# A hybrid decoder layer on one core: alternating two phases' groups, moving the samples' value loads and score transposes, and writing out the matmul engine's loops

## The chip, the cores and the metric

One Trainium2 chip; the program uses one of its cores. The metric is the device time of one execution in microseconds, as the median of several. The engines go by these names: PE is the matmul engine (TensorE; PEld is its weight load), DVE is VectorE, ACT is ScalarE, POOL is GpSimd, SP is the engine that only issues DMAs here.

## What is computed

One step of a decoder layer for 256 prompt tokens and 8 sample tokens that share all weights, T = 264 token columns in all:

```python
h = rmsnorm(x, norm_mix)
parts = jnp.split(h @ w_in, IN_SPLITS, axis=-1)     # u, b_gate, c_gate, q/k/v x 3, gate_a, gate_b
branch_a = (b_gate * causal_dwconv(c_gate * u)) @ w_conv_out
att = attend(qs, ks, vs)                            # samples: over 8 sequences' cached keys and values
branch_b = att.reshape(n, t, ATT_W) @ w_attn_out
x = x + (jax.nn.sigmoid(gate_a) * branch_a + jax.nn.sigmoid(gate_b) * branch_b) @ w_out
h = rmsnorm(x, norm_ffn)
up, gate = jnp.split(h @ w_ffn_in, 2, axis=-1)
x = x + (jax.nn.silu(causal_dwconv(gate) + ffn_conv_b) * up) @ w_ffn_down
```

D_MODEL is 2048, D_CONV 1024, ATT_W 512, D_FF 5632, everything in float32. The new keys, values and convolution states are outputs too.

## The kernel before

**Tiling.** All weights stream once through a ring. The unit is a *chunk*: 256 rows by 512 columns of a weight matrix, 512 KB, in a ring of RING = 4 slots. SP loads it into `raw` (`load`, L292). ACT rounds it to `w_hi` (`hi`, L351, the instruction is on L355), DVE makes the rest `w_lo = raw - w_hi` (`lo`, L550, instruction on L553), and PE multiplies it (`chunk`, L907): for each of four column tiles and two row halves three matmuls of 264 columns (L917 to L919), 24 in a chunk. `his` and `los` run AHEAD = 3 chunks in front of PE. `hi` waits for the landed chunk and for a free slot (`slots_free`, one up for each chunk that PE has finished), `lo` for `hi_ready`, PE for `lo_ready`, and SP's load of chunk s for the split of chunk s - 4.

**Groups.** A *group* is the chunks that make 512 output columns, so four tiles of the accumulator `acc`: eight chunks where the input has 2048 rows (N_MODEL), four for the convolution's output (N_CONV), two for the attention's output (N_ATT). PE can begin a group's tile m only when DVE (or ACT) has taken tile m of the group before (`psum_free`). `take_tiles` (L560) takes tile 0, splits one more chunk, and then takes tiles 1 to 3. The table PHASES (L61) fixes the order of the phases; each engine's program follows it by hand.

**Around the change**, in order of time:

- `ucb`, 48 chunks, written out on all engines; prompt attention is spread between them.
- `gate_a`, four groups in a loop of each engine. In each, DVE also does the samples' scores for two of the eight sequences (L743 to L751): two products and two sums of 1.2 us each over cached keys `k_a`, `k_b` and queries `q_a`, `q_b`. POOL loads them (`load_keys`, L1174, eight DMAs) once the scores of the group before are done, and right behind them the values of the same two sequences (`load_values`, L1185, four DMAs), L1200 to L1203. Behind each group ACT does the sigmoid.
- PE turns the scores (L1041, L1042) as soon as they are complete, before the first group of `conv_out`. DVE and ACT make the softmax of them (L754 to L761, L469).
- `conv_out`, four groups; before the last one PE turns the probabilities back (L1048).
- The samples' attention output: 64 small matmuls with each of `v_a`, `v_b` (L1057).
- `gate_b`, four groups; then `attn_out`, four groups of two chunks. For each of these DVE takes four tiles times `gate_b` into `tf` (L803) and adds `gate_a` (L807), ACT rounds it to `t_hi` (L487), POOL subtracts to `t_lo` (L1211).
- `w_out`, which reads `t_hi` and `t_lo`; then the FFN in two halves (`ffn_a`, `down_a`, `ffn_b`, `down_b`).

On PE all phases but `ucb`, the first third of `qkv` and `attn_out` are in loops (`fetched_loop`, L281): the body stands once in the code and the engine branches back.

Of the kernel before, what the change touches and what calls it, by code (L numbers as in the profile page):

```python
# [26 lines left out]
ALU = mybir.AluOpType  # L27
# [4 lines left out]
D_MODEL = 2048  # L32
# [29 lines left out]
          ("gate_b", 4, N_MODEL), ("attn_out", 4, N_ATT), ("w_out", 4, N_MODEL),  # L62
# [8 lines left out]
CHUNKS = _c  # L71

# [27 lines left out]
def trunk_program(nc, x_fm, w_in, w_conv_out, w_attn_out, w_out, w_ffn_in, w_ffn_down, params, rope_tab,  # L100
                  masks, ident_in, st_mix_in, st_ffn_in, caches, q_new, kv_new,
                  y_out, p_kv, s_kv, conv_state_out, ffn_state_out):
    with ExitStack() as ctx:
# [185 lines left out]
        def _(sp):  # L289
# [34 lines left out]
            with sp.Fori(0, 4) as i:  # L324
                group(w_in, N_MODEL, GW * i + (gate_col + D_MODEL), 2 * i + QUAD0["gate_b"])
            with sp.Fori(0, 2) as i:
                group(w_attn_out, N_ATT, 2 * GW * i, i + QUAD0["attn_out"])
                group(w_attn_out, N_ATT, 2 * GW * i + GW, i + QUAD0["attn_out"], s0=N_ATT)
# [21 lines left out]
        def _(act):  # L350
# [121 lines left out]
            with fetched_loop(mybir.EngineType.Activation, 0, 3) as i:  # L472
                his(i + QUAD0["conv_out"], 0, N_CONV)
# [6 lines left out]
            his(3 + QUAD0["conv_out"], 0, N_CONV)  # L480
            with fetched_loop(mybir.EngineType.Activation, 0, 3) as i:
                gate("gate_b", i, gate_b, gate_b_ready)
            gate("gate_b", 3, gate_b, gate_b_ready, early=1)
# [5 lines left out]
            for j in range(4):  # L489
                if j:  # L490
                    his(QUAD0["attn_out"], N_ATT * j, N_ATT * j + 1)
                    mix_hi(j - 1)
                his(QUAD0["attn_out"], N_ATT * j + 1, N_ATT * (j + 1))
# [55 lines left out]
        def _(dve):  # L549
# [203 lines left out]

            dve.wait_ge(sturned, 2)  # L754
# [7 lines left out]
            with fetched_loop(mybir.EngineType.DVE, 0, 4) as i:  # L762
                los(i + QUAD0["conv_out"], 0, N_CONV - 1)
                dve.wait_ge(gate_a_ready, 4)

                def take_a(m):
                    wait_tile(dve, i + GROUP0["conv_out"], i + QUAD0["conv_out"], N_CONV, m)
                    dve.tensor_tensor(tiles(gate_a, 4 * i + m), acc[:, m:m + 1, 0:T], tiles(gate_a, 4 * i + m),
                                      ALU.mult).then_inc(psum_free, 1)

                take_tiles(take_a, i + QUAD0["conv_out"], N_CONV - 1)
            los(QUAD0["gate_b"], 0, 7)
# [18 lines left out]
            los(2 * 3 + QUAD0["gate_b"], 4, N_MODEL - 1)  # L791
            take_gate("gate_b", 3, gate_b)
            for j in range(4):
                los(QUAD0["attn_out"], N_ATT * j, N_ATT * (j + 1) - 1)
                g = GROUP0["attn_out"] + j
                if j == 0:
                    dve.wait_ge(gate_b_ready, 4)
                if j >= 2:
                    dve.wait_ge(t_ready, j - 1)

                def take_mixed(m):
                    wait_tile(dve, g, QUAD0["attn_out"], N_ATT * (j + 1), m)
                    dve.tensor_tensor(tf[:, j % 2, m, :], acc[:, m, 0:T], gate_b[:, 4 * j + m, :], ALU.mult).then_inc(psum_free, 1)  # L803
# [505 lines left out]
```

## Time and profile before

| | |
|---|---|
| median of 3 runs | 1541.17 us (1539.62 to 1542.80) |
| profiled execution | 1545.92 us, its span 1544.1 us |
| PE busy | 98% |
| DVE, ACT, POOL busy | 58%, 45%, 5% |
| moved by DMA | 307.78 MB, 199 GB/s |
| 512 KB weight load of w_in, issue to landing | 4.1 us (median) |

The span is from the first instruction to the last; the time holds 1.8 us around it. A *busy* PE is one with a matmul in its pipeline; successive matmuls overlap. The *waits* view says for each engine what it stood idle for, and who released it; "issue" means that the profile shows nothing that it waited for. Line numbers are those of the kernel; where a helper records every operation, many phases share one line and are told apart by the tiles' names and by time. The *timeline* lists instructions in order of time, with the idle time before each in brackets. The *windows* view gives the busy time of each engine in a stretch, PE's granted clock (1.00 is 2.4 GHz, 0.50 is 1.2 GHz) and the busy share of the 16 DMA engines.

### The profile page before, as it was taken

What the parts mean: (1) busy time and instruction counts of PE and PEld (TensorE: products, weight loads), DVE (VectorE), ACT (ScalarE), POOL (GpSimd) and SP (SyncE); (2) the same over time, 40 slices, a digit from 0 to 9 for tenths busy, and PEclk for the clock granted to TensorE, in tenths of its full rate; (3) what the DMA queues carried; (4) which work ended last, traced back from release to release, by engine and by line L of the source; (5) the groups of instructions that cost most, each with busy time, mean ns of one, the idle gap of its engine ahead of it and who ended that gap; (6) DMA issues with size and microseconds to landing.
All of it is one profiled execution on the core that took longest, in us unless ns stands there. A gap on an engine that the chain in (4) does not pass through costs nothing.

```text
span 1544.1 us, 32221 instructions
## 1 busy us (share of the span) xinstructions
PE 1514.0 (98%) x12450; PEld 1508.2 (98%) x12450; DVE 893.1 (58%) x1056; ACT 693.0 (45%) x761; POOL 76.3 (5%) x144
## 2 busy tenths in 40 slices
PE   8999999999989999999999999999999999999997
PEld 8999999999988999999999999999999999999996
DVE  8646555756656544675665565663444656556554
ACT  7444444434444344444454444443333444444452
POOL 2000001001230000110000000000000000000000
PEclk9999999999999999999999999999999999999999
DMA  8867576556887665545577776775556565566552
GB/s 278 276 182 247 179 224 189 153 161 198 253 243 207 200 197 170 167 153 200 181 243 250 232 225 219 251 237 169 182 179 179 175 188 180 173 183 195 181 178 97
DMA packets 145108, 307.78 MB, mean 199 GB/s; under 512 B 10112, under 2 KB 10240, under 8 KB 144528
## 3 DMA queue, kind: packets, MB, share of 16 engines
q1 hardware_dynamic: 139120, 268.73, 56.6%
q0 software_dynamic: 5920, 38.12, 7.6%
q8 instruction: 47, 0.77, 0.2%
q14 instruction: 21, 0.17, 0.0%
HBM read 301.39 MB, written 26.38 MB: 212 GB/s over the span
## 4 chain that ended last, share of the span: by engine, by line
PE 95%; DVE 2%; DMA 1%; issue 1%; ACT 1%; SPq 0%; DVEq 0%; ACTq 0%
PE acc L917 31%; PE acc L918 31%; PE acc L919 31%; DMA raw<-w_in 1%; DVE w_lo L553 1%; PE side L1010 1%; PE side L989 1%; ACT w_hi L355 0%; DVE yg L894 0%; PE side L1001 0%; PE side L1057 0%; DVE gate_a L730 0%; DVE tf L803 0%; PE side L976 0%; DVE tf L807 0%
## 5 line engine op out<-in xcount | busy, mean ns | idle before, releaser
L553 DVE TENSOR_TENSOR w_lo<-raw,w_hi 128x1024 fp32r<-128x1024 f32 x503 | 616.8, 1235 | 535.2 <-ACT w_hi L355 532.8
L355 ACT ACTIVATE w_hi<-raw 128x1024 fp32r<-128x1024 f32 x503 | 529.5, 1058 | 728.9 <-PE acc L919 664.2
L917 PE MATMUL acc<-h_hi,w_hi 128*128 128x264 f32 x2872 | 823.6, 287 | 5.9 <-DVE gate_a L730 3.8
L918 PE MATMUL acc<-h_lo,w_hi 128*128 128x264 f32 x2872 | 818.2, 285 | 2.1 <-issue 2.1
L919 PE MATMUL acc<-h_hi,w_lo 128*128 128x264 f32 x2872 | 817.7, 285 | 0.0
L917 PEld LDWEIGHTS acc<-h_hi,w_hi 128*128 128x128 f32 x2872 | 541.3, 188 | 8.2 <-DVE gate_a L730 4.8
L918 PEld LDWEIGHTS acc<-h_lo,w_hi 128*128 128x128 f32 x2872 | 541.4, 189 | 2.4 <-issue 2.3
L919 PEld LDWEIGHTS acc<-h_hi,w_lo 128*128 128x128 f32 x2872 | 541.5, 189 | 0.0
L917 PE MATMUL acc<-f_hi,w_hi 128*128 128x264 f32 x704 | 201.3, 286 | 3.5 <-issue 3.5
L918 PE MATMUL acc<-f_lo,w_hi 128*128 128x264 f32 x704 | 200.8, 285 | 0.0
L919 PE MATMUL acc<-f_hi,w_lo 128*128 128x264 f32 x704 | 200.7, 285 | 0.0
L917 PEld LDWEIGHTS acc<-f_hi,w_hi 128*128 128x128 f32 x704 | 133.0, 189 | 3.7 <-issue 3.7
L918 PEld LDWEIGHTS acc<-f_lo,w_hi 128*128 128x128 f32 x704 | 132.9, 189 | 0.0
L919 PEld LDWEIGHTS acc<-f_hi,w_lo 128*128 128x128 f32 x704 | 132.9, 189 | 0.0
L917 PE MATMUL acc<-t_hi,w_hi 128*128 128x264 f32 x256 | 73.0, 285 | 0.9 <-DVE tf L803 0.9
L918 PE MATMUL acc<-t_lo,w_hi 128*128 128x264 f32 x256 | 72.8, 284 | 0.0
L919 PE MATMUL acc<-t_hi,w_lo 128*128 128x264 f32 x256 | 72.8, 284 | 0.0
L917 PEld LDWEIGHTS acc<-t_hi,w_hi 128*128 128x128 f32 x256 | 48.1, 188 | 1.1 <-DVE tf L803 1.1
L919 PEld LDWEIGHTS acc<-t_hi,w_lo 128*128 128x128 f32 x256 | 48.1, 188 | 0.0
L918 PEld LDWEIGHTS acc<-t_lo,w_hi 128*128 128x128 f32 x256 | 48.1, 188 | 0.0
L918 PE MATMUL acc<-ab_lo,w_hi 128*128 128x264 f32 x128 | 37.0, 289 | 1.0 <-issue 1.0
L917 PE MATMUL acc<-ab_hi,w_hi 128*128 128x264 f32 x128 | 37.5, 293 | 0.5 <-DVE gate_a L730 0.4
(186 smaller groups left out, 841.1 us busy)
## 6 DMA issues: line engine op xcount, KB each, us to landing
raw<-w_in SPq DMA_DIRECT2D x183, 512.0 KB, 4.1
raw<-w_ffn_in SPq DMA_DIRECT2D x176, 512.0 KB, 4.2
raw<-w_ffn_down SPq DMA_DIRECT2D x88, 512.0 KB, 4.5
raw<-w_out SPq DMA_DIRECT2D x32, 512.0 KB, 4.6
s_kv<-cache POOLq DMA_DIRECT2D x16, 1020.0 KB, 8.8
raw<-w_conv_out SPq DMA_DIRECT2D x16, 512.0 KB, 4.7
raw<-w_attn_out SPq DMA_DIRECT2D x8, 512.0 KB, 3.8
s_kv<-cache POOLq DMA_DIRECT2D x8, 508.0 KB, 5.0
```

Of the source, the lines that this page charges most:

```text
L355: act.activation(w_hi[:, s % RING], raw[:, s % RING], ACT.Copy).then_inc(hi_ready, 1)
L553: dve.tensor_tensor(w_lo[:, s % RING], raw[:, s % RING], w_hi[:, s % RING].bitcast(F32), ALU.subtract).then_inc(lo_ready, 1)
L917: pe.matmul(out, w_hi[:, slot, k, cols], backwards(m_hi[:, kt + k, :]), start=first and k == 0, stop=False)
L918: pe.matmul(out, w_hi[:, slot, k, cols], backwards(m_lo[:, kt + k, :]), start=False, stop=False)
L919: mm = pe.matmul(out, w_lo[:, slot, k, cols], backwards(m_hi[:, kt + k, :]), start=False, stop=last and k == 1)
L989: mm = pe.matmul(side[:, SCORES + n * g:SCORES + n * (g + 1)], qkv[:, 12 * g + h, P * qt:P * (qt + 1)], qkv[:, 12 * g + 4 + h, 0:n], start ...
L1010: mm = pe.matmul(side[:, HEAD_OUT:HEAD_OUT + P], vtok[:, kb, (g * HEADS + h) * HEAD_DIM:(g * HEADS + h + 1) * HEAD_DIM], prob_t[:, P * b:P ...
```

## The change

PHASES gets one phase `mix` in place of `gate_b` and `attn_out`. Its eight groups run in the order of WOVEN: second gate 0 and 1, attention 0, gate 2, attention 1, gate 3, attention 2 and 3. SP, ACT, DVE and PE follow this order, written out. A sum is rounded (`mix_hi`) after three chunks' rounding of the next gate group.

In `conv_out`, PE turns the scores behind group 0 and the probabilities behind group 1 (before: ahead of group 0 and behind group 2). DVE does its softmax steps behind group 0, ACT its exponential after five chunks.

POOL loads in the first gate's phase only keys and queries, beside the values of batch 0; batch 1 of the values follows the last scores, batches 2 and 3 follow PE's end of convolution groups 0 and 1.

All loops of PE are written out. The number of matmuls, of bytes and of weight chunks is the same.

```diff
-          ("gate_b", 4, N_MODEL), ("attn_out", 4, N_ATT), ("w_out", 4, N_MODEL),
+          ("mix", 8, (N_MODEL + N_ATT) // 2), ("w_out", 4, N_MODEL),
...
+WOVEN = (("gate_b", 0), ("gate_b", 1), ("attn_out", 0), ("gate_b", 2), ("attn_out", 1), ("gate_b", 3),
+         ("attn_out", 2), ("attn_out", 3))
+MIX_AT = {}
+_c = 0
+for _n, (_name, _j) in enumerate(WOVEN):
+    MIX_AT[_name, _j] = (GROUP0["mix"] + _n, QUAD0["mix"] + _c // RING, _c % RING)
+    _c += N_MODEL if _name == "gate_b" else N_ATT
+assert QUAD0["mix"] + _c // RING == QUAD0["w_out"]
...
+            for name, j in WOVEN:
+                _, quad, s0 = MIX_AT[name, j]
+                if name == "gate_b":
+                    group(w_in, N_MODEL, GW * j + (gate_col + D_MODEL), quad, s0=s0)
+                else:
+                    group(w_attn_out, N_ATT, GW * j, quad, s0=s0)
...
+            his(QUAD0["conv_out"], 0, N_CONV + 1)
             act.wait_ge(smax_ready, 1)
...
+            his(QUAD0["conv_out"], N_CONV + 1, 2 * N_CONV)
             act.wait_ge(pt_zeroed, 2)
             act.wait_ge(spt_done, 2)
...
+            his(QUAD0["conv_out"], 2 * N_CONV, 4 * N_CONV)
...
+            def gate_b_group(j, begun, to_round=None):
+
+                g, quad, s0 = MIX_AT["gate_b", j]
+                if to_round is not None:
+                    his(quad, s0 + begun, s0 + 3)
+                    begun = 3
+                    mix_hi(to_round)
+                his(quad, s0 + begun, s0 + N_MODEL + 1)
+                wait_taken(act, g, TILES - 1)
+                act.activation(gate_b[:, 4 * j:4 * j + 4, :], gate_b[:, 4 * j:4 * j + 4, :], ACT.Sigmoid).then_inc(gate_b_ready, 1)
+
+            def attn_out_group(j, begun):
+                _, quad, s0 = MIX_AT["attn_out", j]
+                his(quad, s0 + begun, s0 + N_ATT)
+
+            gate_b_group(0, 0)
+            gate_b_group(1, 1)
+            attn_out_group(0, 1)
+            gate_b_group(2, 0, to_round=0)
+            attn_out_group(1, 1)
+            gate_b_group(3, 0, to_round=1)
+            attn_out_group(2, 1)
+            his(MIX_AT["attn_out", 3][1], MIX_AT["attn_out", 3][2], MIX_AT["attn_out", 3][2] + 1)
+            mix_hi(2)
+            attn_out_group(3, 1)
...
+            dve.wait_ge(gate_a_ready, 4)
+            conv_group(0)
             dve.wait_ge(sturned, 2)
             dve.tensor_scalar(sprob[:, :], side[0:BATCH * HEADS, 0:SAMPLE_KEYS], -SCALE, None, ALU.mult).then_inc(snegated, 1)
             dve.wait_ge(snegated, 1)
             dve.tensor_reduce(ssmall[:, 0:1], sprob[:, :], AX_X, ALU.min).then_inc(smax_ready, 1)
+            los(QUAD0["conv_out"], N_CONV, N_CONV + 1)
...
+            conv_group(1, begun=1)
+            conv_group(2)
+            conv_group(3)
...
+            def attn_out_group(j):
+                g, quad, s0 = MIX_AT["attn_out", j]
+                los(quad, s0, s0 + N_ATT - 1)
+                dve.wait_ge(gate_b_ready, j + 1)
+                if j >= 2:
+                    dve.wait_ge(t_ready, j - 1)
...
+            gate_b_los(0, 0, 4)
             dve.wait_ge(base_ready, 2)
             dve.wait_ge(shead_done, 1)
             dve.tensor_copy(srows[:, :], side[:, 1024:1024 + HEAD_DIM]).then_inc(srows_ready, 1)
-            take_gate("gate_b", 0, gate_b)
-            with fetched_loop(mybir.EngineType.DVE, 1, 3) as i:
-                los(2 * i + QUAD0["gate_b"], 0, N_MODEL - 1)
-                take_gate("gate_b", i, gate_b)
-            los(2 * 3 + QUAD0["gate_b"], 0, 4)
-
+            gate_b_los(0, 4, N_MODEL - 1)
+            take_gate_b(0)
+            gate_b_los(1, 0, 4)
             dve.wait_ge(sturned_back, 1)
...
-            los(2 * 3 + QUAD0["gate_b"], 4, N_MODEL - 1)
-            take_gate("gate_b", 3, gate_b)
...
+            gate_b_los(1, 4, N_MODEL - 1)
+            take_gate_b(1)
+            attn_out_group(0)
+            gate_b_los(2, 0, N_MODEL - 1)
+            take_gate_b(2)
+            attn_out_group(1)
+            gate_b_los(3, 0, N_MODEL - 1)
+            take_gate_b(3)
+            attn_out_group(2)
+            attn_out_group(3)
...
-            with fetched_loop(mybir.EngineType.PE, 1, NG) as g:
+            for g in range(1, NG):
...
-            with fetched_loop(mybir.EngineType.PE, 0, 4) as i:
+            for i in range(0, 4):
                 h_run(2 * i + QUAD0["gate_a"], i + GROUP0["gate_a"])
+            nbh = BATCH * HEADS
+
+            def conv_group(i):
+                run(i + QUAD0["conv_out"], i + GROUP0["conv_out"], N_CONV, ab_hi, ab_lo)
+
+            pe.wait_ge(ab_ready, 2)
+            conv_group(0)
             pe.wait_ge(scored, 8)
-            pe.transpose(side[0:BATCH * HEADS, 0:ROWS_A], sc_a[:, :], ident[0:ROWS_A, 0:ROWS_A]).then_inc(sturned, 1)
-            pe.transpose(side[0:BATCH * HEADS, ROWS_A:SAMPLE_KEYS], sc_b[:, :], ident[0:ROWS_B, 0:ROWS_B]).then_inc(sturned, 1)
-            pe.wait_ge(ab_ready, 2)
-            with fetched_loop(mybir.EngineType.PE, 0, 3) as i:
-                run(i + QUAD0["conv_out"], i + GROUP0["conv_out"], N_CONV, ab_hi, ab_lo)
+            pe.transpose(side[0:nbh, 0:ROWS_A], sc_a[:, :], ident[0:ROWS_A, 0:ROWS_A]).then_inc(sturned, 1)
+            pe.transpose(side[0:nbh, ROWS_A:SAMPLE_KEYS], sc_b[:, :], ident[0:ROWS_B, 0:ROWS_B]).then_inc(sturned, 1)
+            conv_group(1)
             pe.wait_ge(sprob_ready, 1)
-            nbh = BATCH * HEADS
             pe.transpose(side[0:ROWS_A, 512:512 + nbh], sprob[:, 0:ROWS_A], ident[0:nbh, 0:nbh]).then_inc(spt_done, 1)
             pe.transpose(side[0:ROWS_B, 544:544 + nbh], sprob[:, ROWS_A:SAMPLE_KEYS], ident[0:nbh, 0:nbh]).then_inc(spt_done, 1)
-            run(3 + QUAD0["conv_out"], 3 + GROUP0["conv_out"], N_CONV, ab_hi, ab_lo)
+            conv_group(2)
+            conv_group(3)
...
+            gate_b_group(0)
             pe.wait_ge(srows_ready, 1)
             pe.transpose(side[:, 0:P], srows[:, :], ident[:, :]).then_inc(sturned_back, 1)
-            h_run(2 * 3 + QUAD0["gate_b"], 3 + GROUP0["gate_b"])
+            gate_b_group(1)
             pe.wait_ge(att_ready, 2 * HEADS)
             pe.wait_ge(satt_ready, 1)
-            for j in range(4):
-                run(QUAD0["attn_out"], GROUP0["attn_out"] + j, N_ATT, att_hi, att_lo, s0=N_ATT * j)
-            with fetched_loop(mybir.EngineType.PE, 0, 4) as i:
+            attn_out_group(0)
+            gate_b_group(2)
+            attn_out_group(1)
+            gate_b_group(3)
+            attn_out_group(2)
+            attn_out_group(3)
+            for i in range(0, 4):
...
             ffn_pair("a", 0, stats=1)
-            with fetched_loop(mybir.EngineType.PE, 1, PAIRS_A) as i:
+            for i in range(1, PAIRS_A):
                 ffn_pair("a", i)
-            with fetched_loop(mybir.EngineType.PE, 0, 2) as i:
+            for i in range(0, 2):
                 down("a", i, N_DOWN_A, 0)
-            with fetched_loop(mybir.EngineType.PE, 0, PAIRS_B) as i:
+            for i in range(0, PAIRS_B):
                 ffn_pair("b", i)
-            with fetched_loop(mybir.EngineType.PE, 0, 2) as i:
+            for i in range(0, 2):
                 down("b", i, N_DOWN_B, PAIRS_A)
...
-            with pool.Fori(1, 4) as i:
+            for i in range(1, 4):
                 pool.wait_ge(scored, 2 * i)
                 load_keys(i)
+            pool.wait_ge(scored, 8)
+            load_values(1)
+            for i in range(2, 4):
+                pool.wait_ge(slots_free, RING + 4 * QUAD0["conv_out"] + N_CONV * (i - 1))
                 load_values(i)
 
 
-            pool.wait_ge(slots_free, RING + 4 * QUAD0["gate_b"])
+            pool.wait_ge(slots_free, RING + 4 * QUAD0["mix"])
```

## Rows read from the trace of the kernel before

**Rows 1.** Page, its span, and busy time by engine: share, instructions
```profile
span 1544.1 us, 32221 instructions
...
PE 1514.0 (98%) x12450; PEld 1508.2 (98%) x12450; DVE 893.1 (58%) x1056; ACT 693.0 (45%) x761; POOL 76.3 (5%) x144
```

**Rows 2.** Waits of PE: line <- releaser: us in total, times, longest
```profile
PE acc L917 <- DVE gate_a L730: 4.2, 4, 2.8
PE acc L917 <- issue: 4.0, 2, 3.5
PE acc L918 <- issue: 3.1, 2, 2.1
PE acc L917 <- DVE tf L803: 2.1, 3, 0.9
PE side L1041 <- DVE sc_b L749: 1.8, 1, 1.8
PE acc L917 <- DVE w_lo L553: 1.5, 2, 1.2
```

**Rows 3.** Timeline of PE: start, us, instruction [idle before it <- releaser]
```profile
453.82 0.28 PE L919 MATMUL acc<-h_hi,w_lo 128*128 128x264 f32 x1
...
456.93 0.39 PE L917 MATMUL acc<-h_hi,w_hi 128*128 128x264 f32 x1 [2.82 <-DVE gate_a L730]
...
484.59 0.28 PE L1041 MATMUL side<-ident,sc_a 128*32 128x128 f32 x1 [1.80 <-DVE sc_b L749]
...
612.37 0.49 PE L918 MATMUL acc<-h_lo,w_hi 128*128 128x264 f32 x1 [2.07 <-issue]
...
1043.12 0.59 PE L917 MATMUL acc<-f_hi,w_hi 128*128 128x264 f32 x1 [3.46 <-issue]
```

**Rows 4.** Windows: length, PE, PEld, DVE, ACT, POOL busy (x), PEclk, DMA share, GB/s
```profile
225.00:376.00 151.00, 151.00 (x1242) 150.38 (x1241) 91.86 (x139) 66.43 (x86) 12.71 (x25) 1.00 0.62 185
388.00:405.00 17.00, 17.00 (x142) 17.00 (x142) 12.78 (x12) 6.36 (x6) 2.67 (x6) 1.00 0.84 252
458.90:462.30 3.40, 3.40 (x18) 3.40 (x17) 0.13 (x1) 3.05 (x3) 3.05 (x7) 0.50 0.81 233
1047.00:1180.00 133.00, 133.00 (x1098) 133.00 (x1098) 60.12 (x59) 48.72 (x46) 0.00 (x0) 1.00 0.57 175
```

**Rows 5.** Timeline of POOL, loads of the third key and value batch
```profile
433.80 0.51 POOL L1183 DMA_DIRECT2D q_b<-q_new  x1
...
436.54 0.58 POOL L1190 DMA_DIRECT2D v_b<-kv_new  x1 [0.21 <-issue]
```

**Rows 6.** DMA issues, window 430 to 450: KB each, us to landing
```profile
raw<-w_in SPq DMA_DIRECT2D x5, 512.0 KB, 10.6
...
q_b<-q_new POOLq DMA_DIRECT2D x1, 12.0 KB, 10.3
...
v_b<-kv_new POOLq DMA_DIRECT2D x1, 12.0 KB, 11.7
```

**Rows 7.** Timeline of ACT, window 448 to 449
```profile
448.56 1.06 ACT L355 ACTIVATE w_hi<-raw 128x1024 fp32r<-128x1024 f32 x1 [7.54 <-DMA raw<-w_in]
```

**Rows 8.** Timeline of DVE, windows 456 to 457 and 486 to 492
```profile
456.46 0.42 DVE L730 TENSOR_TENSOR gate_a<-acc,r 128x264 f32 x1
...
491.51 0.15 DVE L759 RECIPROCAL ssmall<-ssmall 32x1 f32<-32x1 f32 x1 [3.81 <-ACT sprob L470]
```

**Rows 9.** Timeline of DVE and POOL, window 645 to 649
```profile
646.62 2.40 DVE L553 TENSOR_TENSOR w_lo<-raw,w_hi 128x1024 fp32r<-128x1024 f32 x1
...
645.49 2.44 POOL L1211 TENSOR_TENSOR t_lo<-tf,t_hi 128x1056 fp32r<-128x1056 f32 x1 [109.03 <-ACT t_hi L487]
```

**Rows 10.** Instruction queue: packets, MB, share; page, then 226:376 and 1038:1090
```profile
q8 instruction: 47, 0.77, 0.2%
...
q8 instruction: 9, 0.15, 0.4%
...
q8 instruction: 5, 0.08, 0.6%
```

More of the change, by code:

```diff
@@ L752, in _, with conv_group, take_a @@
                 take_gate("gate_a", i, gate_a)
+            def conv_group(i, begun=0):
+                quad = QUAD0["conv_out"]
+                los(quad, N_CONV * i + begun, N_CONV * (i + 1) - 1)
+                def take_a(m):
+                    wait_tile(dve, i + GROUP0["conv_out"], quad, N_CONV * (i + 1), m)
+                    dve.tensor_tensor(tiles(gate_a, 4 * i + m), acc[:, m:m + 1, 0:T], tiles(gate_a, 4 * i + m),
+                                      ALU.mult).then_inc(psum_free, 1)
+                take_tiles(take_a, quad, N_CONV * (i + 1) - 1)
+            dve.wait_ge(gate_a_ready, 4)
+            conv_group(0)
             dve.wait_ge(sturned, 2)
@@ L761, in _, with take_gate_b, take, gate_b_los @@
             dve.tensor_scalar(sprob[:, :], sprob[:, :], ssmall[:, 2:3], None, ALU.mult).then_inc(sprob_ready, 1)
[L762 to L772, printed above, removed]
+            conv_group(1, begun=1)
+            conv_group(2)
+            conv_group(3)
+            def take_gate_b(j):
+                g, quad, s0 = MIX_AT["gate_b", j]
+                def take(m):
+                    wait_tile(dve, g, quad, s0 + N_MODEL, m)
+                    dve.tensor_tensor(gate_b[:, 4 * j + m, :], acc[:, m, 0:T], r[:, :], ALU.mult).then_inc(psum_free, 1)
+                take_tiles(take, quad, s0 + N_MODEL - 1)
+            def gate_b_los(j, first, last):
+                _, quad, s0 = MIX_AT["gate_b", j]
+                los(quad, s0 + first, s0 + last)
+            def attn_out_group(j):
[4 more added lines that the diff above has]
+                    dve.wait_ge(t_ready, j - 1)
+                def take_mixed(m):
+                    wait_tile(dve, g, quad, s0 + N_ATT, m)
+                    dve.tensor_tensor(tf[:, j % 2, m, :], acc[:, m, 0:T], gate_b[:, 4 * j + m, :], ALU.mult).then_inc(psum_free, 1)
+                take_tiles(take_mixed, quad, s0 + N_ATT - 1)
+                wait_taken(dve, g, TILES - 1)
+                dve.tensor_tensor(tf[:, j % 2], tf[:, j % 2], gate_a[:, 4 * j:4 * j + 4, :], ALU.add).then_inc(mixed, 1)
+            gate_b_los(0, 0, 4)
             dve.wait_ge(base_ready, 2)
@@ L1060, in _, with gate_b_group, attn_out_group @@
             mm.then_inc(shead_done, 1)
[L1061 to L1062 removed]
+            def gate_b_group(j):
+                g, quad, s0 = MIX_AT["gate_b", j]
+                h_run(quad, g, s0=s0)
+            def attn_out_group(j):
+                g, quad, s0 = MIX_AT["attn_out", j]
+                run(quad, g, N_ATT, att_hi, att_lo, s0=s0)
+            gate_b_group(0)
             pe.wait_ge(srows_ready, 1)
             pe.transpose(side[:, 0:P], srows[:, :], ident[:, :]).then_inc(sturned_back, 1)
[L1065 removed]
+            gate_b_group(1)
             pe.wait_ge(att_ready, 2 * HEADS)
             pe.wait_ge(satt_ready, 1)
[L1068 to L1070 removed]
+            attn_out_group(0)
[5 more added lines that the diff above has]
+            for i in range(0, 4):
                 run(2 * i + QUAD0["w_out"], i + GROUP0["w_out"], N_MODEL, t_hi, t_lo,
```

31 lines of the change are left out of this document (removed).

## The prediction

> **What bounds the kernel now.** I read the page first. The matmul engine is busy for 98% of the span and no other engine for more than 58% [rows 1]; the chain that ended last is 95% matmuls. So only two things can shorten this kernel: fewer matmuls, or fewer pauses between them. The change leaves every matmul in place, so I counted the pauses. Second view: the waits of the matmul engine [rows 2]. They sum to 16.7 us in six lines, and the list is short enough to place each one in time with the engine's timeline [rows 3]. Two conversions are needed. A matmul is listed with 0.28 us but the next one starts 0.12 us after it, so a listed idle time is 0.16 us short of what is lost: 453.82 to 456.93 is 3.11 us, 2.99 more than the usual 0.12, and 2.82 are listed [rows 3]. And after the longer pauses the granted clock is at half: from 458.9 to 462.3 the window shows 0.50 (the 1.2 GHz level), with 18 matmuls, those at its edges counted, where full speed (1098 in 133 us, 0.121 us each) has 28 [rows 4]. Some 16 matmuls take 3.4 us instead of 1.9, so 1.5 us per such stretch. There are four: behind the pauses that end at 456.93 and 458.40, at 484.59 and 486.40, at 612.37, and at 1043.12. The six lines with their 14 pauses' 0.16 us each, and the four stretches, are 16.7 + 2.2 + 6.0 = 24.9 us: about that is what any reordering can win. 1.2 us of w_lo and 0.5 us of issue in them lie in the first 36 us, which the change doesn't touch.
>
> **The change part by part.**
>
> *Values' loads.* In each of the first gate's groups 1 to 3, GpSimd issues eight key and query loads and behind them four value loads, 844 KB; in group 2 the last of the first kind at 433.80, the last of the second at 436.54 [rows 5]. They sit in the same 16 DMA engines as the weights. In 430 to 450 us a 512 KB weight load takes 10.6 us to land; the last value load lands 11.7 us after its issue, at 448.2 [rows 5, 6]. ScalarE waits 7.54 us for that weight chunk and starts on it at 448.56 [rows 7]. VectorE then has three chunks to split and four key steps to do back to back, and comes to the gate's tiles only at 456.46 [rows 8]; the matmul engine has nowhere to write from 454 on. Without the values, what landed with and after the keys comes earlier by the values' own transfer. Bounds: 844 KB at the 252 GB/s that 388 to 405 carried is 3.3 us [rows 4]; the last value at 448.2 against the last query piece at 433.80 + 10.3 = 444.1 is 4.1 us [rows 5, 6]. I take 4.1, as it is measured between two landings. VectorE is then at the gate's first tile at 452.4, a tile that the matmul engine needs at 453.9, so the 2.99 us go, and with them the smaller pauses around it. Listed idle of this stage: three of the four "gate_a" waits (4.2 less the 0.42 of 486.40) and 0.27 of w_lo, 4.1 us; plus 4 x 0.16 and 0.3 us of a pause too short to be listed: 5.0 us. Plus one half-clock stretch: 6.5 us. With 3.3 instead of 4.1 us some 0.8 us stays. Where the loads go: batch 1 now starts at the end of the key steps, batches 2 and 3 one and two groups into the convolution's output. There the price is bounded by the one place where a value batch runs without keys today: at 387 us; the matmul engine had no idle time in 388 to 405 [rows 4]. I take nothing, and the same 3 to 5 us as above as the other end. The last batch is issued two groups (23 us) ahead of its use and took at most 11.7 us to land, so the wait for the values stays empty. GpSimd's next job, the load of x, waits for the same point as before.
>
> *Score transposes later.* Today the matmul engine waits for the last score sum, starts the transposes at 484.59 after 1.80 us of listed idle, 1.97 lost, and then pauses twice more, for 0.85 us in all, for a tile that VectorE frees late [rows 2, 3]. With a group of the convolution (11.7 us) put in front, the score sums are long done: 1.97 + 0.85 + a half-clock stretch of 1.4 = 4.2 us. The two transposes still run. In the new order VectorE's softmax steps come after group 0: ScalarE's exponential holds VectorE for 3.81 us today [rows 8], but behind that wait is queued only the split of the chunk that group 2 starts with, some 11 us before it is needed; the probabilities are needed one group later too. Cost nothing; if that cover were missing, 3.8 us.
>
> *The matmul engine's loops written out.* Three pauses have no releaser ("issue"): 1.0 us in the convolution's loop, 2.07 us right after the second gate's loop is left (it ends at 612.37), 3.46 us right after the first FFN loop is left (it ends at 1043.12) [rows 2, 3]. The DMA queue of the instruction blocks (16 KB each) has 47 packets over the span: five of them in 1038 to 1090, just behind the first FFN loop [rows 10]. Straight code is in the trace too: the 48 chunks from 225 to 376 us take nine blocks in 151 us, which would be 91 over 1531 us, and the engine is busy for all of it [rows 4, 10]. So a loop that repeats fetches next to nothing, and the code behind it is fetched only when the loop is left, and whether that stalls depends on how much of it is already there. Written out, every block is fetched ahead like those: 1.0 + 2.07 + 3.46 + 3 x 0.16 = 7.0 us, and two half-clock stretches, 3.0: 10.0 us. The Trainium skill ("Runtime: NRT & Kernel Launch", section "Instruction fetch mechanics") has the same rule: the matmul engine's buffer is refilled in 16 KiB blocks ahead of use, purely in sequence, and a taken branch to a block that isn't there forces a fetch before execution goes on. The rows of the two loop exits agree. The 1.0 us inside the convolution's loop might by the rows alone be another's, and the sum 1.2 us less; by the rule it is a late block too.
>
> *Alternating groups.* An attention group has only two chunks, 5.8 us of matmuls. Four in a row leave VectorE no room: two splits, four tiles and a sum are 5.2 us when undisturbed, and a split beside GpSimd's subtraction (645.49 to 647.93) took 2.40 us instead of 1.23 [rows 9]. Three pauses follow, 2.1 us listed, 2.6 us in truth [rows 2]. Between groups of the second gate (eight chunks, 23.3 us, in which VectorE has eight splits of 1.23 us and four tiles) the rounding and GpSimd's subtraction fall where there is slack. The last two attention groups still stand together, with GpSimd's subtraction beside the second, so one pause of 0.5 us remains, now ahead of the output projection: 2.1 us gained. New waits: the first attention group needs the samples' attention after gate group 1 instead of 3; its steps are queued behind the fifth chunk of that group, some 9 us ahead. VectorE waits for each sigmoid by group, and each is at least one group old, but for the last, which has the third attention group as cover (5.8 us for about 3). Cost nothing.
>
> **Sum.** 6.5 + 4.2 + 10.0 + 2.1 = 22.8 us. Profiled execution 1545.92 us (span 1544.1 and 1.8 around it): 1523.1 us. The median of the runs shown is 4.75 us below the profiled one. Either recording costs that much outside the pauses, then it stays, 1518.4; or the unrecorded runs have less of the pauses, then part of the gain isn't there, 1523.1. I take the middle: 1520.5 us; its own range is 1516 to 1526.
>
> **The rivals.**
> 1. *The values disturb the convolution's output.* By the Trainium skill ("DMA: Bandwidth & Descriptors", section "Issuing engines are not separate DMA queues") loads of all issuers interleave on the same 16 engines, so moving one only moves the crowd. In this kernel: batch 1 is issued right behind the last keys' backlog, and the convolution's weights need 180 GB/s (512 KB in 2.9 us) with 72 GB/s more from the values (844 KB in 11.7 us). For it: the second gate-a group shows that a burst can cost 5 us. Against it: 252 GB/s was carried in 388 to 405 without a pause [rows 4]. Price: one pause of 3 us and a half-clock stretch, 4.5: 1525.
> 2. *The "issue" pauses are not the loops'*, or come back elsewhere. For it: nine loops are left, and only three pauses show. Price: the 10.0 us stay: 1530.5.
> 3. *Slower: straight code whose blocks come late.* Written out, the engine needs a block every 17 us all along, some 91 instead of 47, also under GpSimd's key loads with the DMA engines 0.8 busy and more; the straight code of 225 to 376 had them at 0.62 [rows 4]. A late block costs what the three did, 2 to 3.5 us and 1.5 for the clock, 4.2 on average. The rest of the change saves 12.8, so from 4 late blocks on the kernel is slower than before: with seven, 1541.2 - 12.8 + 29.4 = 1557.8. Against it: nine blocks without a wait, and each transfer took about 1 us.
> 4. *The woven groups pause*: a wait in front of or behind each lone attention group, the price of the largest pause there today, 1.1 us, four times: 2.1 gained become 2.3 lost: 1525.
>
> **How the numbers follow.** Forecast 0.70, rival 1 0.09, rival 2 0.10, rival 3 0.04, rival 4 0.04, other 0.03. The range goes from 1515.5 (all pauses gone and 3 us more beside the part that recording explains) to 1529 (rivals 1 and 4 in; rival 2 mostly out). A measurement of this kernel can tell about 0.2%, 3.1 us, from no change. Faster by more: all but rival 3 and part of "other", 0.93; within 0.03; slower 0.04.
>
> **What would show it.** In the changed kernel's profile: no "issue" waits of the matmul engine beyond the 0.5 us near 32 us, and 90 to 100 packets in the queue of the instruction blocks; no wait for gate_a tiles from the first gate on, ScalarE's waits for weights there down from 7.5 to about 3.5 us; the score transposes with no wait ahead; at most one wait for tf; and PEclk at 1.00 from 5 us to the end but for stretches that a pause explains. The prediction is wrong if the count of instruction blocks rises and "issue" waits rise with it, if weight loads in the convolution's output take over 9 us to land, or if the pauses vanish but the median falls by less than 15 us, which would mean that they belonged to the recording.

## The result, and the profile after

The changed kernel takes 1522.96 us (median of 4, 1521.77 to 1525.36) against 1541.99 us (4 runs, 1539.62 to 1544.24): 19.0 us less, ratio 0.9879, 95% interval 0.9859 to 0.9899. Profiled execution against profiled execution it is 1521.96 against 1545.92 us, 24.0 less. The prediction was 1520.5 us and, for the profiled one, 1523.1. One of all the runs below, of the changed kernel with its loops put back, took 2102.28 us at a mean granted clock of 0.65 against 1529 to 1532 us of its others, and is left out.

The page of the changed kernel, its span, engines, granted clock (tenths, 40 slices) and the queue of the matmul engine's instruction blocks:

```profile
span 1520.4 us, 31542 instructions
...
PE 1505.6 (99%) x12450; PEld 1502.7 (99%) x12450; DVE 891.6 (59%) x1056; ACT 686.7 (45%) x756; POOL 77.4 (5%) x144
...
PEclk9999999999999999999999999999999999999998
...
q8 instruction: 99, 1.62, 0.4%
```

The waits of PE in it (us in total, times, longest), complete. They answer to [rows 2], where six lines had 14 waits, the sc_b one among them (two more of the view, 1.3 and 0.9 us, lie in its first 12 us):

```profile
PE acc L971 <- DVE w_lo L581: 2.0, 1, 2.0
PE side L1014 <- POOL ones L1175: 1.3, 1, 1.3
PE acc L971 <- DVE tf L831: 0.4, 1, 0.4
```

The first two are the start, before 12 us. Between 36 us and the end one wait of 0.4 us is left, the one ahead of the output projection. The gate_a, sc_b and issue lines are gone, and with them all four half-clock stretches. The blocks fetched went from 47 to 99.

Where the time came from is seen in the first gate. ScalarE's wait for weights there, and VectorE's arrival at the tiles of groups 2 and 3 of the gate (timelines of ACT and DVE):

```profile
442.33 1.06 ACT L366 ACTIVATE w_hi<-raw 128x1024 fp32r<-128x1024 f32 x1 [2.57 <-DMA raw<-w_in]
...
449.10 1.21 DVE L777 TENSOR_REDUCE sc_b<-k_b 83x1024 f32 x1
450.51 0.43 DVE L758 TENSOR_TENSOR gate_a<-acc,r 128x264 f32 x1 [0.21 <-PE acc L973]
...
472.31 1.21 DVE L777 TENSOR_REDUCE sc_b<-k_b 83x1024 f32 x1
473.82 0.43 DVE L758 TENSOR_TENSOR gate_a<-acc,r 128x264 f32 x1 [0.30 <-PE acc L973]
```

Before, ScalarE waited 7.54 us [rows 7] and VectorE took the tile at 456.46 without having waited for it [rows 8]. Now it is VectorE that waits for the matmul engine, at 450.51 and at 473.82. The last score sum starts at 472.31 instead of 483.3, and the window shows no idle time at all in a stretch that still moves 252 GB/s (length, busy PE, PEld, DVE, ACT, POOL, granted clock, DMA share, GB/s):

```profile
425.00:490.00 65.00, 65.00 (x538) 64.97 (x538) 43.84 (x50) 33.65 (x32) 13.81 (x24) 1.00 0.86 252
```

The value batches now land under the convolution's output. In 487 to 512 us its weight loads take 6.3 us to land (median of six), more than the 4.7 of the kernel before (median of all sixteen), and the matmul engine has no wait there:

```profile
raw<-w_conv_out SPq DMA_DIRECT2D x6, 512.0 KB, 6.3
...
v_a<-cache POOLq DMA_DIRECT2D x2, 512.0 KB, 5.9
```

### The profile page after: what moved, and what is told of

Same layout as the page of the kernel before. It is cut to its first block, busy times and chain, and to the rows that moved or that the text cites. A ratio compares the mean times of both kernels' runs of the same rounds, so it can differ in the third digit from the quotient of the medians.

```text
span 1520.4 us, 31542 instructions
## 1 busy us (share of the span) xinstructions
PE 1505.6 (99%) x12450; PEld 1502.7 (99%) x12450; DVE 891.6 (59%) x1056; ACT 686.7 (45%) x756; POOL 77.4 (5%) x144
## 4 chain that ended last, share of the span: by engine, by line
PE 98%; DVE 1%; DMA 0%; SPq 0%; ACT 0%; issue 0%; DVEq 0%
PE acc L971 32%; PE acc L972 32%; PE acc L973 32%; PE side L1064 1%; PE side L1043 1%; DMA raw<-w_in 0%; DVE yg L948 0%; PE side L1055 0%; PE side L1116 0%; DVE w_lo L581 0%; PE side L1030 0%; DVE r L623 0%; PE side L1169 0%; ACT w_hi L366 0%; PE side L1002 0%; SPq L316 0%
```

## The experiments

The first two, the fourth and the fifth do one part of the change alone on the kernel before, the third does two parts together; then come two runs that move nothing but the place of the code, and parts undone. Each time is given beside runs of the kernel before on the same chip. These had medians of 1542.09, 1546.35 and 1545.12 us in the three series of these runs, so differences from different series can be off by some microseconds; the profiled executions all stand against the one of the kernel before, 1545.92.

### The loops written out, alone

```diff
-            with fetched_loop(mybir.EngineType.PE, 1, NG) as g:
+            for g in range(1, NG):
...
```

and likewise all others of PE.

> The kernel before with only the matmul engine's loops written out. Theory (the code behind a loop is fetched late): the three issue pauses of 1.0, 2.07 and 3.46 us and two half-clock stretches go, 8.5 to 10 us less than before in the profiled execution, some 99 instruction blocks instead of 47; the gate_a, sc_b and tf waits stay as they are. Rival (the pauses are not the loops'): they stay or move, and the time is within 2 us of before. Rival (straight code is fetched late where the DMA engines are full, 400 to 480 us, since keys and values are still loaded together here): new issue pauses of 2 to 3.5 us there.

Measured: 1535.71 us against 1542.09, ratio 0.9955 (0.9938 to 0.9973): 6.4 us less; profiled 1532.88, which is 13.0 below the 1545.92 of before. Its waits of PE:

```profile
PE acc L917 <- DVE gate_a L730: 4.3, 4, 2.9
PE acc L917 <- DVE tf L803: 2.1, 3, 0.9
PE acc L917 <- DVE w_lo L553: 1.9, 2, 1.5
PE side L960 <- POOL ones L1104: 1.3, 1, 1.3
PE acc L933 <- DVE w_lo L604: 0.3, 1, 0.3
PE acc L917 <- issue: 0.2, 1, 0.2
```

All three issue pauses behind loops are gone, none is new in 400 to 480 us, and the gate_a and tf lines are nearly those of [rows 2]. The sc_b wait is gone as well, though this edit doesn't touch it: the last sum began at 482.00 us instead of 483.33, and the matmul engine came some 0.7 us later, since its half-clock stretch in the gate was twice as long here (456.4 to 463.1 us, with 27 matmuls). That is 2 of the 3 us by which the profiled execution gained more than the 8.5 to 10 expected. So the pauses were the loops', and straight code isn't late even with keys and values on the DMA engines. The median moved less than the profiled execution did; that is taken up below.

### The values moved, alone

```diff
-            with pool.Fori(1, 4) as i:
+            for i in range(1, 4):
                 pool.wait_ge(scored, 2 * i)
                 load_keys(i)
+            pool.wait_ge(scored, 8)
+            load_values(1)
+            for i in range(2, 4):
+                pool.wait_ge(slots_free, RING + 4 * QUAD0["conv_out"] + N_CONV * (i - 1))
                 load_values(i)
```

> The kernel before with only the value batches 1 to 3 moved behind the scores and into the convolution's output. Theory (values hold up the weights): ScalarE's longest wait for weights in the first gate falls from 7.5 to about 3.5 us, the gate_a pauses (5.0 us) and the half-clock stretch behind them go, and part of the wait for the last score sum, since that comes 4 us earlier too: 6.5 to 10 us less. The issue pauses stay. Rival (the keys alone are enough to hold up the weights): the 2.82 us pause stays at over 1.5 us, under 4 us are gained. Rival (the values now disturb the convolution's output): a pause and half-clock stretch there, 4.5 us back.

Measured: 1538.43 us against 1542.09, ratio 0.9964 (0.9947 to 0.9981): 3.7 us less, and the profiled execution, 1543.33, only 2.6. Its waits of PE, and the instruction behind the longest:

```profile
PE acc L918 <- issue: 8.1, 2, 6.3
PE acc L917 <- issue: 3.6, 2, 3.2
PE acc L917 <- DVE w_lo L553: 2.6, 2, 1.4
PE acc L917 <- DVE tf L803: 2.2, 3, 0.9
PE side L960 <- POOL ones L1104: 1.3, 1, 1.3
```
```profile
486.43 0.38 PE L918 MATMUL acc<-ab_lo,w_hi 128*128 128x264 f32 x1 [6.34 <-issue]
```

No gate_a and no sc_b line: this part alone removes all of what I had booked under the values and under the score transposes. But the pause in the convolution's loop, 1.0 us before, is now 6.34 us, and a half-clock stretch of 6.8 us begins towards its end; so most of the gain is lost again. The trace has the instruction queue's packet, one of 16 KB. In the kernel before it goes from 488.59 to 489.47 us and the matmul engine goes on at 491.06. Here the last matmul starts at 479.81, the packet goes from 483.89 to 484.91, and the next matmul starts at 486.43. Value batch 1 was issued from 475 us on, and the packet starts just when the DMA engines have become empty (length, busy PE, PEld, DVE, ACT, POOL, granted clock, DMA share, GB/s):

```profile
480.00:483.80 3.80, 0.09 (x1) 0.00 (x0) 1.03 (x3) 3.17 (x5) 0.00 (x0) 1.00 0.88 189
483.80:486.00 2.20, 0.00 (x0) 0.00 (x0) 0.66 (x1) 0.00 (x0) 0.00 (x0) 0.74 0.18 40
```

That speaks for the block having stood in line behind the values; when it was asked for isn't in the trace. The convolution's output is disturbed then, as the first rival said, but by way of the code, not of the weights.

### Loops written out and values moved

> The kernel before with two parts together: the matmul engine's loops written out and the value batches moved. Apart they gave 6.4 us and 3.7 us. Theory (with loops, the value batch that now runs under the convolution's loop holds up that loop's late code block, 6.3 us; written out, the block is fetched ahead): no issue pause over 0.5 us, no gate_a pause, together 14 to 17 us less than before, more than the sum of 10.1. Rival (the parts just add up): 10 us. Rival (the values also delay blocks of straight code): issue pauses of over 1 us between 475 and 510 us.

Measured: 1524.62 us against 1546.35, ratio 0.9860 (0.9845 to 0.9875): 21.7 us less, twice the 10.1 of the two apart. Waits of PE, complete:

```profile
PE acc L917 <- DVE tf L803: 2.2, 3, 0.9
PE acc L917 <- DVE w_lo L553: 1.6, 1, 1.6
PE side L960 <- POOL ones L1104: 1.3, 1, 1.3
PE acc L933 <- DVE w_lo L604: 0.3, 1, 0.3
PE acc L917 <- issue: 0.3, 1, 0.3
```

More than I had expected, 14 to 17. Each part takes away what spoils the other: in the written-out code no block is late, so the values can't hold one up. The size of that surplus is less sure. The same kernel, run once more on the chip of the single parts, was 19.5 us below the kernel before. In the profiled executions the parts give 13.0 + 2.6 = 15.6 us apart and 21.6 together, and the 6.0 between them is near what the traces list: a code pause longer by 5.3 us and half-clock stretches worth 3.0 us that the single parts kept and the two together don't have, less the 2.0 us of the sc_b wait, which both single parts lost. What the medians show beyond that isn't explained.

### The scores' transposes moved, alone

On PE (the convolution's first group in front; the probabilities stay behind group 2), with VectorE's and ScalarE's order as in the change:

```diff
+            run(QUAD0["conv_out"], GROUP0["conv_out"], N_CONV, ab_hi, ab_lo)
             pe.wait_ge(scored, 8)
             pe.transpose(side[0:BATCH * HEADS, 0:ROWS_A], sc_a[:, :], ident[0:ROWS_A, 0:ROWS_A]).then_inc(sturned, 1)
...
-            with fetched_loop(mybir.EngineType.PE, 0, 3) as i:
+            with fetched_loop(mybir.EngineType.PE, 1, 3) as i:
```

> The kernel before with only the score transposes and the softmax steps put behind the convolution's group 0 (probabilities still turned behind group 2). Theory of the sum: the wait of 1.80 us for the last score sum goes, the pause for a gate_a tile at the first convolution group stays or grows, since VectorE is as late as before (its last score sum ends at 484.5 and the tiles of the gate come after it): 1 to 2 us gained, not 4.2. If the 4.2 us are this part's own: 3.5 us or more gained. Rival (VectorE's softmax steps in front of the next splits become late): a w_lo wait in the convolution's output, slower by 1 to 3 us.

Measured: 1534.89 us against 1542.09, ratio 0.9946 (0.9930 to 0.9962), 7.2 us less. By the time alone the second case, the part being worth 4.2 us of its own, would seem right. The waits of PE tell otherwise:

```profile
PE acc L926 <- DVE gate_a L730: 6.2, 5, 2.8
PE acc L926 <- DVE w_lo L553: 2.3, 2, 2.1
PE acc L926 <- DVE tf L812: 2.2, 3, 0.9
PE side L969 <- POOL ones L1114: 1.3, 1, 1.3
PE acc L942 <- DVE w_lo L604: 0.7, 1, 0.7
PE acc L926 <- issue: 0.3, 1, 0.3
```

The sc_b wait of 1.8 us has become a gate_a wait of about the same length (4.2 in [rows 2], 6.2 here). So the transposes' place took no pause away; at most the half-clock stretch goes to its credit that stood behind the sc_b wait (486.3 to 489.6 us) and isn't there in this run (granted clock 1.00 in 484 to 496 us). What fell is the 6.5 us of issue pauses, of which 0.3 is left. They stood behind the first gate's, the second gate's and the first FFN loop, which this edit doesn't touch. It takes one pass out of the convolution's loop and so puts 96 matmuls and their weight loads more into the code.

### The groups alternating, alone

The change's mix phase with everything else of the kernel before, PE's other loops included.

> The kernel before with only the second gate's and the attention output's groups alternating; their code is written out on all engines, all other loops of the matmul engine stay. Theory: of three tf pauses of 2.1 us listed one of about 0.4 stays, 2.1 us gained; and as the second gate's loop is gone, the issue pause of 2.07 us and its half-clock stretch go too, 3.8 us: about 6 us less than before. Rival (lone attention groups pause): tf or gate_b waits at each of them, only the 3.8 us gained or less.

Measured: 1538.48 us against 1542.09, ratio 0.9975 (0.9958 to 0.9992): 3.6 us less, where about 6 had been expected; the profiled execution is 7.6 us below. The tf line is down to one wait, as predicted, and with the second gate's loop its pause has gone. The pause behind the first FFN loop is still there, and that in the convolution's loop is 1.8 us instead of 1.0 (L963). The gate stage has its gate_a waits; the sc_b wait isn't there, as in the run with the loops, though neither touches what it waits for:

```profile
PE acc L962 <- DVE w_lo L581: 4.9, 2, 3.0
PE acc L962 <- DVE gate_a L758: 4.0, 3, 1.9
PE acc L963 <- issue: 1.8, 1, 1.8
...
PE acc L962 <- DVE tf L822: 0.4, 1, 0.4
```

The w_lo line hides the pause behind the first FFN loop, 3.46 us in the kernel before: at 1035.11 us the matmul engine had been idle for 3.01 us, and the view names a split that ended at 1034.65. But that one belongs to the chunk three further on; the one that the engine went on with was split before 1028.7.
### Nothing moved but the place of the code

The run with the scores alone made it a question why loops pause at all, so here nothing of the work is changed. 128, in another run 64 instructions that only count up an unused semaphore stand in front of PE's code:

```diff
             pe.sem_inc(psum_free, TILES)
+            for _ in range(128):
+                held(pe)
```

> The kernel before with 128 instructions that do nothing (an unused semaphore counted up) put in front of the matmul engine's code, half an instruction block. Theory (whether leaving a loop stalls depends on where its end lies in the blocks): the three issue pauses (1.0 us at 490, 2.07 at 612, 3.46 at 1043) change in size, or vanish, or come behind other loops; everything else stays, apart from a start that is later by the time of the 128. Rival (they belong to a place in the work, a semaphore or a DMA): the same three pauses within 0.5 us each at the same places.

> The kernel before with 64 instructions that do nothing in front of the matmul engine's code (half of the run with 128, where the start came 17.6 us later and, of the pauses at 490, 612 and 1043, none was left and one of 1.1 us stood 22 us into the third FFN phase's surroundings, at 1189). Theory (place of the code in the blocks): again another set of issue pauses, start some 9 us later. Rival (the late start, not the place of the code, took the pauses away): no set of its own, the same as with 128.

Each was run once: 1557.62 us with 128 (the kernel before: 1546.35 on that chip) and 1554.98 with 64 (1545.12). With 128 the start comes late (20.9 us of issue before the first matmul), and between 640 us and the end the waits of PE are

```profile
PE acc L919 <- DVE tf L803: 2.2, 3, 0.9
PE acc L920 <- issue: 1.1, 1, 1.1
```

The pauses of 1.0, 2.07 and 3.46 us are gone; one of 1.1 us stands at 1190.52, behind the first down projection's loop, which had none. With 64 there are three long ones, at the ends of the qkv loop and of the first FFN loop, and 3 us into the code behind the second FFN loop:

```profile
228.90 0.39 PE L919 MATMUL acc<-h_hi,w_hi 128*128 128x264 f32 x1 [2.38 <-issue]
...
1046.05 0.58 PE L919 MATMUL acc<-f_hi,w_hi 128*128 128x264 f32 x1 [4.08 <-DVE f_lo L865]
...
1426.33 0.29 PE L921 MATMUL acc<-f_hi,w_lo 128*128 128x264 f32 x1 [2.48 <-issue]
```

The 4.08 us are named after VectorE's `f_lo`, but the first chunk of the down projection needs only the first pair's, which was done 230 us earlier.

That another set of pauses isn't just another execution is seen from the runs whose matmul engine has the same code up to the pause: the kernel before, the run with the values alone and the one with the groups alone all pause at the same matmul of the convolution's first pass (for 1.0, 6.3 and 1.8 us), and the first two also at the same ones behind the second gate's and the first FFN loop (2.1 and 1.8, 3.5 and 3.2 us). So the place goes with the code, the length varies.

And what the engine lacks is in the traces. Fifteen pauses of 0.7 us and more stand behind loops in the traces of the kernel before, of the values alone, of the groups alone, of both padded kernels and of the loops put back. In each, one 16 KB packet of the instruction queue ended 1.3 to 1.9 us before the matmul that ended the pause.

So the pauses belong neither to a semaphore nor to a stage of the work, nor to a late start: they go with how the code lies in its blocks. That explains the issue pauses that came and went in the single parts. An edit that adds or removes instructions ahead of a loop can draw the pauses behind all later loops anew. The Trainium skill ("Runtime: NRT & Kernel Launch", section "Instruction fetch mechanics") says that a taken branch whose target isn't in the current window forces a fetch before execution can continue. The traces agree that a fetch is waited for; the fifteen pauses all came within 30 matmuls behind a loop's last pass, and none at a branch back. With 0, 64 and 128 instructions in front their sum is 6.5, 8.9 and 1.1 us with the same work.

### The loops put back into the changed kernel

> The changed kernel with the matmul engine's loops put back where the order of groups still allows them (first third aside: qkv, first gate, output projection, FFN and down projections). Theory: one or more issue pauses of 1 to 6 us, at the convolution behind the first gate's loop (the value batch lands there) and behind an FFN loop, each over 2 us with a half-clock stretch of 1.5 us: 4 to 10 us slower than the changed kernel, but in the traces with loops pauses come and go with the place of the code, so it can also hit none, then 0 to 1 us. Rival (loops cost nothing, other parts made the gain): within 1.5 us of the changed kernel and no issue pause.

Measured: 1529.21 to 1532.49 us against 1546.35, ratio 0.9896 (0.9880 to 0.9912) to the kernel before. The changed kernel stands at 0.9879 in one series and 0.9861 in another, so the loops cost 2.6 to 5.4 us here, at the lower end of the 4 to 10 expected; the interval still overlaps that of 0.9879. Two of their waits of PE, and the longest in its place, the end of the second FFN loop:

```profile
PE acc L971 <- issue: 4.1, 3, 3.0
...
PE acc L973 <- issue: 1.0, 1, 1.0
```
```profile
1395.76 0.39 PE L971 MATMUL acc<-f_hi,w_hi 128*128 128x264 f32 x1 [3.03 <-issue]
```

### The values put back into the changed kernel

> The changed kernel with the value batches back beside the keys in the first gate. Theory: gate_a or w_lo pauses of 4 to 5 us in all and a half-clock stretch between 425 and 485 us, 5 to 8 us slower than the changed kernel, and no issue pause, since straight code is fetched ahead even there. Rival (straight code is late where the DMA engines are full): issue pauses of over 1 us between 400 and 480. Rival (the late score sum was what mattered): under 3 us slower.

Measured: 1533.56 us against 1546.35, ratio 0.9920 (0.9907 to 0.9934), which is 6.3 us more than by the changed kernel's 0.9879 and 9 more than by its 0.9861; expected were 5 to 8. The waits of PE and the longest wait of ScalarE for weights:

```profile
PE acc L971 <- DVE gate_a L758: 6.4, 4, 2.8
...
PE acc L971 <- issue: 0.4, 1, 0.4
```
```profile
ACT w_hi L366 <- DMA raw<-w_in: 30.3, 17, 6.9
```

All the pauses of the gate stage return with the values, also the one ahead of the convolution's output, now named gate_a instead of sc_b, and two half-clock stretches with them. The 0.4 us of issue is the one near 32 us, as before the change: straight code, keys and values together, and no late block.

### The transposes put back; and the changed kernel beside it

> The changed kernel once more, on the chip of the next three, as their measure. All four parts. Expected 21 to 24 us below before on this chip, no issue pause over 0.5 us and one tf pause of 0.4 us.

> The changed kernel with the score transposes and the softmax steps back in their old places, the loops written out all the same. Theory formed from the run with loops and values alone, which had no wait for the last score sum: with the values out of the way that sum is done some 9 us before the transposes, so this part is worth nothing of its own; within 1 us of the changed kernel, no sc_b wait. Rival (the prediction's sum, in which the part has 4.2 us of its own): a pause of 1 to 2 us at the start of the convolution's output, and 3 us or more slower.

> The kernel before with loops written out and values moved, once more beside the changed kernel, so that what the other two parts add is measured on one chip. Theory: the two tf pauses of 0.9 us each and the small one moved elsewhere, 2.1 us; scores nothing: 1.5 to 2.5 us slower than the changed kernel. Rival (lone attention groups cost what they save): within 0.7 us.

Measured on one chip, where the kernel before takes 1545.12 us:

| kernel | us | ratio (95%) |
|---|---|---|
| the changed kernel | 1522.32 | 0.9861 (0.9843 to 0.9879) |
| with the transposes in their old place | 1523.35 | 0.9865 (0.9844 to 0.9886) |
| loops and values only | 1525.64 | 0.9884 (0.9865 to 0.9903) |

The second has no sc_b wait and no pause in the convolution's output; profiled it takes 1523.44 against the changed kernel's 1523.79. The transposes' place is worth nothing once the values are moved, or less than these runs can tell. The third is 2.3 us behind the second (1.1 in the profiled executions), about the size of the two tf waits and their 0.16 us each, though the intervals overlap, so the times alone don't show it. Its traces name those waits:

```profile
PE acc L917 <- DVE tf L803: 2.1, 3, 0.9
```

## Why the prediction was right, and where it wasn't

**What bounds the kernel, and the count of pauses.** Right. The matmul engine is still the bound, 24.9 us were counted as what reordering can win, and 23.7 us of span went.

**Values' loads, 6.5 us.** Right in mechanism, too small in size. ScalarE's wait fell from 7.54 to 2.57 us (2.63 at the longest in any group of the gate), VectorE came to the tile with time to spare, and the lower bound's left-over of 0.8 us didn't show. What was mis-sized is what hangs on it: the sc_b wait and the pauses behind it, listed under the next part, are gone with the values alone. With the loops written out the values are worth 8.6 us in the profiled executions (1532.88 to 1524.29), and put back they cost 10.7 there (1532.64 against 1521.96) and 6.3 to 9 by the ratios.

**Score transposes, 4.2 us.** The step that failed. The pauses at the start of the convolution's output came from the same cause as those of the gate: the last score sum was late because the weights were. With the values moved and the transposes in their old place, that sum starts at 473.80 us, takes 1.2, and the transposes run at 477.17 without a wait: 2 us to spare (the 9 us in that run's expectation were wrong). Alone, the transposes' move only turned the 1.8 us wait into a gate_a wait; undone, it changed nothing beyond 1 us. The sum stayed right because 6.5 + 4.2 = 10.7 us is about what the values gave, 8.6 to 10.7 profiled. That is luck: I had priced the second stage's pauses as if the first hadn't been mended, and gave them to a part that earns nothing. The sc_b wait isn't even steady: it was 1.8 us in the kernel before, 2.5 in both padded kernels and absent in the runs with the loops or the groups alone.

**Loops written out, 10.0 us.** Right for this profiled execution: all three pauses went, alone and in the whole, and 99 blocks were fetched, where 90 to 100 had been foretold. The 1.0 us in the convolution's loop, which the prediction left open by its rows, is a late block too: its packet ended 1.6 us before the matmul at 491.06. But the pauses are not a constant of the kernel before. Of the loops' part alone, 13.0 us show in the profiled execution and 6.4 us in the median. And I missed how this part and the values depend on each other: apart 6.4 and 3.7 us, together 21.7 and, on the other chip, 19.5.

**Alternating groups, 2.1 us.** Right by the traces: 2.1 us listed became 0.4, in the place and of the size foretold, and no wait stands at the lone attention groups. The 2.3 us between the two kernels that differ in it have the right size, but lie within the noise.

**Profiled execution and median.** The 4.75 us between them in the kernel before were split in the middle between "recording costs it" and "the pauses vary". What the runs show speaks for the second: in the runs before, times spread over 1536.8 to 1549.6 us, while the changed kernel's lie in 1521.8 to 1525.4, and its recorded runs are 1.0 us below and 1.5 above their medians. The mean granted clock of the 38 runs before in the three series goes with their times: the 16 at 0.992 and 0.993 took 1545.4 us on average, the two at 0.997 took 1537.0. So the number of half-clock stretches, and of pauses in front of them, differs from one execution to the next; with the pauses gone the spread is gone. Which pauses vary was seen in no second trace of the same kernel. An unrecorded run had less of them to lose: hence 19.0 us less in the median against 24.0 profiled, and 1523 instead of 1520.5.

**The rivals.** The first (values disturb the convolution's output) happens, but only with loops left in, and through a code block instead of weights: 6.34 us at its worst. The second (the issue pauses aren't the loops') falls with the loops' own run and the padded ones. The third (straight code late) falls: no issue wait over 0.5 us in 1500 us of straight code, even with the values back in the gate. The fourth is refuted by the tf line.

**Open.** Why a given place of a loop in the blocks pauses for 1.0, 2.07 or 3.46 us, and another doesn't, wasn't worked out; the three placements show only that it does, and each padded kernel has only one trace. Nor was the alternation tried with the transposes moved but the values not.

## What to carry to other kernels

Before adding up the pauses of a bound engine, ask of each which earlier one made it: two of mine had one cause, and the sum was right only since both went. A loop on the engine that sets the time can stall at its end by some microseconds, at a place that any edit to the code ahead of it moves, and longer when a burst of other DMA stands in front of the missing block; where the program isn't too long, write that engine's loops out before measuring anything else, or each measurement carries that draw. And put bulk loads into a stage where the ring of weights has no other bulk load beside it, rather than right behind the keys that the same stage waits for.

## What the runs showed of the hardware

- Behind a loop's end the matmul engine paused for 0.7 to 4.1 us until an instruction block was there, and for 6.3 us with 844 KB of value loads in the DMA engines. The block's packet took 0.9 to 1.1 us, and the next matmul started 1.3 to 1.9 us after it. In straight code, with 99 such 16 KB blocks, there was no such pause.
- 128 semaphore increments in front of the matmul engine's code delayed its first matmul until 20.9 us after its start, 64 until 11.1 us: by the difference 0.15 us each.
- VectorE's split next to GpSimd's subtraction takes 2.40 us instead of 1.23 in the changed kernel too. By the alternation two of GpSimd's four subtractions (at 587.57 and 616.72 us) run beside groups of the gate, where nobody waits. This split is the one beside the last attention group, and the one wait left, 0.4 us at 644.76, comes behind it:

```profile
641.97 2.40 DVE L581 TENSOR_TENSOR w_lo<-raw,w_hi 128x1024 fp32r<-128x1024 f32 x1
```
